# Moving some expert-weight loads from SyncE's DMA queue to ScalarE's in a two-layer hybrid backbone with a mixture of experts

## The chip, the cores and the metric

The kernel runs on one core of a Trainium2 chip. The metric is the device time of one execution, in microseconds (us). Five engines work side by side, each through its own list of instructions: TensorE (PE, matmuls), VectorE (DVE), ScalarE (ACT), GpSimd (POOL) and SyncE (SP, which here only issues DMA transfers). Semaphores order them against each other. DMA transfers are carried out by 16 DMA engines of the core; who issues a transfer decides through which queue it reaches them.

## The reference, cut to what matters

Two layers. Each is a token mixer (convolution, attention, RWKV-7 and retention heads, not touched here), then an expert-choice mixture of experts over 1024 latent tokens, and in the first layer over 256 context tokens as well. Everything is float32.

```python
def route_set(hs):
    aff = jax.nn.softmax((hs @ w_router + b_router).astype(jnp.float32), axis=-1)
    gate, idx = lax.top_k(aff.T, cap)              # 16 experts; cap = 128 latent tokens each
    xe = hs[idx]
    hid = jax.nn.silu(jnp.einsum('ecd,edf->ecf', xe, w_gate)) * jnp.einsum('ecd,edf->ecf', xe, w_up)
    ye = jnp.einsum('ecf,efd->ecd', hid, w_down) * gate[..., None].astype(hid.dtype)
    return jnp.zeros(hs.shape, ye.dtype).at[idx.reshape(-1)].add(ye.reshape(-1, hs.shape[-1]))
```

`w_gate`, `w_up` and `w_down` are 1024 x 1024 for each of 16 experts and each of two layers: 12 MB of weights for an expert, used once.

## The kernel before, in words

The work that the change touches is `stage_moe`, which runs once in each layer over the experts e = 0 to 15. An expert's three matrices are cut into quarters of 1 MB: g11, g12, g21, g22 of the gate matrix, u11 to u22 of the up matrix, d0 to d3 of the down matrix. All quarters pass through `g.moe_w`, a ring of 16 places in SBUF. `MOE_PARTS` lists them in the order of loading: for an expert g11, u11, g21, u21, g12, u12, g22, u22, and then d0 to d3 of the expert before. Part j goes to place j modulo 16, so it can be loaded only when part j - 16 has been used up. In steady state this gives, while expert e is computed: g12 and u12 of e+1 follow g11 and u11 of e; g22 and u22 of e+1 follow g21 and u21; d0 and d1 of e follow g12 and u12; d2 and d3 of e follow g22 and u22; and g11, u11, g21, u21 of e+2 follow d0 to d3 of e-1.

Gate and up projections are done with seven products of half-size blocks (Strassen-Winograd) in place of eight. TensorE runs them in the order P1, P2 | P6, P5, P7, P4, P3 (`first_products` and `other_products`, each product eight matmul pairs at L2915). The last reader of the quarters 11 is P5, of 12 is P7, of 21 is P4, of 22 is P3. Each product reads a gate and an up quarter at once, so both come free together. TensorE's list for expert e is: P6, four transposes, P5, four transposes of the next expert's tokens, P7, P4, P3, then P1 and P2 of expert e+1, then (first layer only) the context tokens' products of e+1, then eight transposes of the hidden rows of e (`hidden_turned`, L2958), then the down projection of e (L3014), which reads d0, d1, d2, d3 in this order.

ScalarE copies partial products and transposed tokens out of PSUM and applies SiLU (`gate`); VectorE forms the sums of weights and tokens that the products need (L3143, L3113), joins partial products (L3149) and multiplies gate and up (L3155). GpSimd gathers each expert's tokens and scatters its results with indirect DMAs.

Before the change every weight quarter is loaded by SyncE, in the order of `MOE_PARTS`, each behind a wait for its place:

```python
for j in range(RW, len(MOE_PARTS)):
    name, eo = MOE_PARTS[j - RW]
    if name[0] == "d":
        ...
    else:
        sp.wait_ge(*product_at(eo, {"11": P5, "12": P7, "21": P4, "22": P3}[name[1:]]))
    load_expert_part(sp, g, I, l, j)
```

The first 16 quarters of a layer are loaded by SyncE in `stage_topk`, ahead of this loop.

Of the kernel before, what the change touches and what calls it, by code (L numbers as in the profile page):

```python
# [86 lines left out]
def linker(eng, sig):  # L87

    def link(ins):
        ins.then_inc(*sig.up())  # L90
        eng.wait_ge(sig.sem, sig.made)
    return link
# [80 lines left out]
def row(v):  # L173

    return v.partition_broadcast(P)
# [2504 lines left out]
MOE_PARTS = [(name, e + d) for e in range(NE + 1) for name, d in MOE_ORDER if 0 <= e + d < NE]  # L2680
PART_AT = {part: j for j, part in enumerate(MOE_PARTS)}


def load_expert_part(sp, g, I, l, j):

    name, e = MOE_PARTS[j]
    half, c = divmod(int(name[1]), 2) if name[0] == "d" else (int(name[1]) - 1, int(name[2]) - 1)
    src = I[{"g": "w_gate", "u": "w_up", "d": "w_down"}[name[0]]][l, e].rearrange("(k p) f -> p k f", p=P)
    sp.dma_start(g.moe_w[:, j % MOE_RW], src[:, 4 * half:4 * half + 4, 512 * c:512 * c + 512]).then_inc(*g.sg(f"w_slot{j % MOE_RW}").up(16))  # L2689
# [75 lines left out]
def stage_moe(nc, g, I, l, need_ctx):  # L2765
# [4 lines left out]
    RW, w = MOE_RW, g.moe_w  # L2770
    A_, B_, C_, D_, CB, CD, YB = 0, 1, 2, 3, 4, 5, 6
    P1, P2, P6, P5, P7, P4, P3 = range(1, 8)
# [3 lines left out]
    with ExitStack() as cx:  # L2776
# [38 lines left out]
        def product_at(e, p):  # L2815

            return pm.at(7 * e + p)

        def joined_at(e, c):

            return cd.at(4 * e + c)
# [5 lines left out]
        def out_of(c):  # L2827

            return cb[:, {C11: 0, C12: 0, C21: 1, C22: 1}[c], {C11: 0, C21: 0, C12: 1, C22: 1}[c]]

        with nc.Block() as block:
            @block.sync
            def _(sp):
                sp.dma_start(rows[:], row(g.mod[l, 0, 5 * D:6 * D])).then_inc(*small.up(16))
                if need_ctx:
                    for q in range(4):
                        sp.dma_start(rowc[32 * q:32 * q + 32], g.mod[l, 1, 5 * D + 256 * q:5 * D + 256 * q + 256].partition_broadcast(32)) \
                            .then_inc(*small.up(16))
                for j in range(RW, len(MOE_PARTS)):
                    name, eo = MOE_PARTS[j - RW]  # L2840
                    if name[0] == "d":
                        if need_ctx:
                            sp.wait_ge(*dmc.at(eo + 1))
                        else:
                            sp.wait_ge(*dm.at(4 * eo + int(name[1]) + 1))
# [3 lines that stand above are left out]
# [182 lines left out]
            @block.scalar  # L3031
            def _(act):
                link = linker(act, achain)

                def x_copy(e, half):
                    act.wait_ge(*xtr.at(2 * e + half + 1))
                    nc.scalar.copy(xT[:, e % 2, 4 * half:4 * half + 4].rearrange("p k n -> p (k n)"), ps[:, C_]).then_inc(*xte.up())  # L3037

                def c_copy(e):
                    act.wait_ge(*xtrc.at(e + 1))  # L3040
                    nc.scalar.copy(xTc[:].rearrange("p k n -> p (k n)"), ps[:, CD, 256:256 + KT * CAPC]).then_inc(*xtec.up())

                def partial(e, p, i):
                    act.wait_ge(*product_at(e, p))
                    if p == P1 and e:
                        act.wait_ge(*joined_at(e - 1, C21))
                    if p == P6 and e:
                        act.wait_ge(*joined_at(e - 1, C12))
                    if p == P7:
                        act.wait_ge(*joined_at(e, C11))  # L3050
                    nc.scalar.copy(part[:, i], ps[:, A_]).then_inc(*tcd.up())  # L3051

                def gate(e, c):
                    act.wait_ge(*joined_at(e, c))
                    r, n = (0, 0) if c == C11 else (0, 1) if c == C12 else (1, 0) if c == C21 else (1, 1)
                    return nc.scalar.activation(hid[HF * r:HF * r + HF, 512 * n:512 * n + 512], out_of(c)[0:HF], ACT.Silu)

                def context_copy(e):
                    act.wait_ge(*cgu.at(e + 1))
                    nc.scalar.copy(gu[:], ps[:, CB]).then_inc(*cev.up())  # L3060

                def context_gate(e):
                    act.wait_ge(*ctr.at(e + 1))
                    if e:
                        act.wait_ge(*dmc.at(e))
                    nc.scalar.activation(hTc[:], ps[:, CB].rearrange("p (i q n) -> p i q n", i=4, q=4)[:, :, 0:2], ACT.Silu).then_inc(*cgs.up())

                x_copy(0, 0)
                x_copy(0, 1)
                if need_ctx:  # L3070
                    c_copy(0)
                partial(0, P1, 0)
                if need_ctx:
                    context_copy(0)
                    context_gate(0)
                for e in range(NE):
                    more = e + 1 < NE
                    partial(e, P6, 1)
                    if more:
                        x_copy(e + 1, 0)  # L3080
                        x_copy(e + 1, 1)
                        if need_ctx:
                            c_copy(e + 1)
                    partial(e, P7, 0)
                    gate(e, C11)
                    link(gate(e, C22))
                    link(gate(e, C21))
                    nc.scalar.copy(out_of(C21)[0:HF], out_of(C11)[HF:P]).then_inc(*hs.up())
                    gate(e, C12)
                    nc.scalar.copy(out_of(C22)[0:HF], out_of(C12)[HF:P]).then_inc(*hs.up())  # L3090
                    if more:
                        partial(e + 1, P1, 0)
                        if need_ctx:
                            context_copy(e + 1)
                    for half in range(2):
                        act.wait_ge(*htr.at(2 * e + half + 1))
                        nc.scalar.copy(hT2[:, 4 * half:4 * half + 4].rearrange("p k n -> p (k n)"), ps[:, C_ + half]).then_inc(*he.up())  # L3097
                    if more and need_ctx:
                        context_gate(e + 1)
# [226 lines left out]
```

## Time and profile before

| | |
|---|---|
| median of 3 runs | 4143.54 us (4136.83 to 4148.22) |
| the profiled execution's own time | 4128.93 us |
| its span | 4127.1 us |
| busy: PE, DVE, ACT, POOL | 3651.8, 2224.7, 1062.2, 491.2 us |
| experts' stage, first layer | about 1434 to 2228 us of the span |
| experts' stage, second layer | about 3489 to 4116 us of the span |
| weight quarters loaded in the two stages | 384 of 1 MB |

A row of the chain or of a timeline gives the start in us from the span's start, the length in us, and what ran; a bracket tells how long the engine had been idle before it and what ended that. "SPq" is SyncE issuing a DMA: its length is the time the issue took, not that of the transfer. The rows of a view of the DMA queues give how many packets each queue moved, their size, and the share that their time is of 16 engines' time; an issue's row ends with the us from issue to landing. Queue q1 holds what SyncE issues, q0 what GpSimd issues.

### The profile page before, as it was taken

What the parts mean: (1) busy time and instruction counts of PE and PEld (TensorE: products, weight loads), DVE (VectorE), ACT (ScalarE), POOL (GpSimd) and SP (SyncE); (2) the same over time, 40 slices, a digit from 0 to 9 for tenths busy, and PEclk for the clock granted to TensorE, in tenths of its full rate; (3) what the DMA queues carried; (4) which work ended last, traced back from release to release, by engine and by line L of the source; (5) the groups of instructions that cost most, each with busy time, mean ns of one, the idle gap of its engine ahead of it and who ended that gap; (6) DMA issues with size and microseconds to landing.
All of it is one profiled execution on the core that took longest, in us unless ns stands there. A gap on an engine that the chain in (4) does not pass through costs nothing. (4 is left out here: it accounts for less than half of the span.)

```text
span 4127.1 us, 65802 instructions
## 1 busy us (share of the span) xinstructions
PE 3651.8 (88%) x27258; PEld 2030.6 (49%) x27258; DVE 2224.7 (54%) x3676; ACT 1062.2 (26%) x2344; POOL 491.2 (12%) x675
## 2 busy tenths in 40 slices
PE   6899999677897699999997899998697875999998
PEld 4555575566733233333333655674486532333333
DVE  2454224687755644444443445334778757565654
ACT  3342010544311111111112443112534221212121
POOL 1100000221201011111111200000232110110100
PEclk8999999688998799999998899999698987999999
DMA  6300120200175677777774000121100326999996
GB/s 229 125 1 11 56 77 0 79 13 19 44 278 206 228 261 261 262 261 262 262 255 120 33 21 11 59 69 36 54 10 13 114 103 250 329 333 330 333 329 204
DMA packets 291447, 613.12 MB, mean 149 GB/s; under 512 B 37544, under 2 KB 45992, under 8 KB 284496
## 3 DMA queue, kind: packets, MB, share of 16 engines
q1 hardware_dynamic: 270608, 542.32, 36.9%
q0 software_dynamic: 20544, 66.60, 6.3%
q8 instruction: 219, 3.59, 0.4%
q14 instruction: 76, 0.62, 0.0%
HBM read 561.07 MB, written 47.79 MB: 148 GB/s over the span
## 5 line engine op out<-in xcount | busy, mean ns | idle before, releaser
L3014 PE MATMUL ps<-moe_w,e_hT 128*128 128x512 f32 x1024 | 451.1, 598 | 17.4 <-issue 9.2
L3143 DVE TENSOR_TENSOR moe_w<-moe_w 128x2048 f32<-128x2048 f32 x128 | 287.1, 2285 | 204.0 <-PE ps L2945 159.2
L2915 PE MATMUL ps<-moe_w,e_xs 128*64 128x512 f32 x1536 | 348.6, 596 | 0.8 <-DVE moe_w L3143 0.8
L2915 PE MATMUL ps<-moe_w,e_xT 128*64 128x512 f32 x1536 | 343.7, 597 | 0.7 <-DVE moe_w L3143 0.7
L3014 PEld LDWEIGHTS ps<-moe_w,e_hT 128*128 128x128 f32 x1024 | 192.9, 191 | 255.5 <-issue 252.7
L3149 DVE TENSOR_TENSOR e_cb<-e_part,ps 128x512 f32<-128x512 f32 x128 | 87.7, 685 | 335.2 <-ACT e_part L3051 249.3
L2915 PEld LDWEIGHTS ps<-moe_w,e_xT 128*64 128x64 f32 x1536 | 111.4, 138 | 221.3 <-issue 221.2
L2915 PEld LDWEIGHTS ps<-moe_w,e_xs 128*64 128x64 f32 x1536 | 105.4, 137 | 193.7 <-issue 192.3
L1207 PE MATMUL ps<-M 96*128 96x512 f32 (+1 forms) x400 | 182.6, 543 | 3.5 <-PEq L913 2.1
L3051 ACT COPY e_part<-ps 128x512 f32<-128x512 f32 x96 | 56.3, 586 | 479.8 <-PE ps L2915 471.5
L1097 PE MATMUL ps<-yT,hT 128*128 128x272 f32 (+1 forms) x608 | 146.6, 396 | 9.6 <-PEq L262 9.2
L659 ACT COPY yT<-ps 128x256 f32<-128x256 f32 (+1 forms) x90 | 42.5, 472 | 402.7 <-PE ps L571 402.7
L3143 DVE TENSOR_TENSOR moe_w<-e_t,moe_w 128x2048 f32<-128x2048 f32 x64 | 143.5, 2283 | 0.0
L1219 PEld LDWEIGHTS ps<-all_tabs,a_pr 128*128 128x128 f32 x656 | 74.7, 142 | 129.5 <-issue 88.2
L1097 PEld LDWEIGHTS ps<-yT,hT 128*128 128x128 f32 x608 | 114.7, 195 | 41.4 <-issue 20.0
L3143 DVE TENSOR_TENSOR e_t<-moe_w 128x2048 f32<-128x2048 f32 x60 | 134.5, 2283 | 0.0
L1219 PE MATMUL ps<-all_tabs,a_pr 128*128 128x128 f32 x656 | 111.9, 284 | 20.2 <-ACT a_pt L1268 13.8
L1268 DVE COPY a_pt<-ps 128x512 f32<-128x512 f32 (+1 forms) x104 | 61.1, 588 | 127.3 <-PE ps L1219 126.9
L2877 POOL DMA_INDIRECT x_rows<-e_ye,all_tok x16 | 52.6, 3290 | 641.1 <-DVE e_ye L3184 641.1
L1283 DVE TENSOR_REDUCE a_mx<-ps 128x1 f32<-128x1280 f32 (+1 forms) x72 | 98.4, 1367 | 52.2 <-PE ps L1207 52.2
L2877 POOL DMA_INDIRECT out_dram<-e_ye,all_tok x16 | 52.2, 3264 | 593.9 <-DVE e_ye L3184 593.9
L1310 ACT ACTIVATE a_pr<-ps,a_mx 128x1280 f32<-128x1280 f32 (+1 forms) x72 | 88.8, 1233 | 112.9 <-DVE a_mx L1284 112.9
(424 smaller groups left out, 7093.8 us busy)
## 6 DMA issues: line engine op xcount, KB each, us to landing
moe_w<-in_w_gate_dram SPq DMA_DIRECT2D x128, 1024.0 KB, 13.9
moe_w<-in_w_up_dram SPq DMA_DIRECT2D x128, 1024.0 KB, 14.1
moe_w<-in_w_down_dram SPq DMA_DIRECT2D x128, 1024.0 KB, 13.0
o_mod_w<-in_w_ada_dram SPq DMA_DIRECT2D x24, 1024.0 KB, 7.9
m_mod_w<-in_w_ada_dram SPq DMA_DIRECT2D x16, 1024.0 KB, 5.8
yT<-in_w_in_dram SPq DMA_DIRECT2D x6, 2048.0 KB, 7.9
r_z<-z_rows SPq DMA_DIRECT2D x20, 512.0 KB, 3.4
z_rows<-p_zo POOLq DMA_DIRECT2D x36, 256.0 KB, 2.3
```

The lines of the kernel that those rows point to most:

```text
L1097: ins = nc.tensor.matmul(ps[:, ZBANK[a], 0:hi - lo], hT[:, k, t * P:(t + 1) * P], w[:, k, lo:hi], start=(k == 0), stop=(k == KT - 1))
L1207: ins = nc.tensor.matmul(ps[:, SB[u % 2] + i, 0:w], QT[0:QK, h, t * P:(t + 1) * P], KTr[0:QK, h, n:n + w], start=True, stop=True)
L1219: ins = nc.tensor.transpose(ps[:, TB, k * P:(k + 1) * P], pr[:, u % NP, (k0 + k) * P:(k0 + k + 1) * P], g.ident)
L1268: copy(pt[:, k % 2, u % 2, k0:k0 + nk].rearrange("p k n -> p (k n)"), ps[:, TB, 0:nk * P]).then_inc(*done.up())
L1283: link(nc.vector.reduce_max(mx[:, s % 2, 0:1], src, AX_X))
L1310: nc.scalar.activation(pr[:, s % NP, 0:units[s][2] * P], src, ACT.Exp, bias=mx[:, s % 2, 1:2], scale=SCALE, accum_out=rs[:, s // 2 % 4, s ...
L2877: pool.indirect_dma_start(dst, bass.IndirectOffsetOnAxis(ap=g.tok[:, 0, e:e + 1], axis=0), ye[:], None, compute_op=ALU.add).then_inc(*sc.u ...
L2915: ins = nc.tensor.matmul(ps[HF * q:HF * q + HF, b, :], x[:, k], weights[q][:, k], start=(first and k == 0), stop=(k == 3), skip_group_chec ...
L3014: ins = nc.tensor.matmul(ps[:, YB + c, :], hT2[:, 4 * half + k], quarter(name, e)[:, k], start=(half == 0 and k == 0), stop=(half == 1 and ...
L3051: nc.scalar.copy(part[:, i], ps[:, A_]).then_inc(*tcd.up())
L3143: nc.vector.tensor_tensor(to, a, b, ALU.subtract).then_inc(*td.up())
L3149: nc.vector.tensor_tensor(out_of(c), part[:, 1 if c == C12 else 0], ps[:, b], ALU.subtract if c == C21 else ALU.add).then_inc(*cd.up())
```

## The change

SyncE's loop skips every part whose place was held by an up quarter. ScalarE issues those loads itself, at the point of its list where that quarter's last reader has run: `refill(e, "u11")` behind the copies of the next expert's transposed tokens, `refill(e, "u12")` behind the copy of P7, `refill(e, "u21")` behind the third SiLU, `refill(e, "u22")` behind the fourth. In steady state the loads moved are u12 and u22 of e+1 and d1 and d3 of e; d0, d2, all gate quarters and u11, u21 of e+2 stay with SyncE. These are 60 loads in each layer. No other work, buffer or size changes.

```diff
@@ SyncE's loop
                 for j in range(RW, len(MOE_PARTS)):
                     name, eo = MOE_PARTS[j - RW]
+                    if name[0] == "u":
+                        continue
                     if name[0] == "d":
@@ ScalarE's list
+                def refill(e, name):
+                    j = PART_AT[name, e] + RW
+                    if j < len(MOE_PARTS):
+                        act.wait_ge(*product_at(e, {"u11": P5, "u12": P7, "u21": P4, "u22": P3}[name]))
+                        load_expert_part(act, g, I, l, j)
+
@@
+                    refill(e, "u11")
                     partial(e, P7, 0)
+                    refill(e, "u12")
                     gate(e, C11)
                     link(gate(e, C22))
                     link(gate(e, C21))
+                    refill(e, "u21")
                     nc.scalar.copy(out_of(C21)[0:HF], out_of(C11)[HF:P]).then_inc(*hs.up())
                     gate(e, C12)
+                    refill(e, "u22")
                     nc.scalar.copy(out_of(C22)[0:HF], out_of(C12)[HF:P]).then_inc(*hs.up())
```

SyncE's list in the second layer, one expert in steady state, before. moe_w1 is the ring of quarters; signal29 counts the products of gate and up, signal11 those of the down projection. The loads are g12, u12, g22, u22, then d0 to d3, then g11, u11, g21, u21:

```order
L2689 DMA moe_w1<-in_w_gate_dram 128x4x512 [waits signal29]
L2689 DMA moe_w1<-in_w_up_dram 128x4x512 [waits signal29]
L2689 DMA moe_w1<-in_w_gate_dram 128x4x512 [waits signal29]
L2689 DMA moe_w1<-in_w_up_dram 128x4x512 [waits signal29]
L2689 DMA moe_w1<-in_w_down_dram 128x4x512 [waits signal29] x4
L2689 DMA moe_w1<-in_w_gate_dram 128x4x512 [waits signal11]
L2689 DMA moe_w1<-in_w_up_dram 128x4x512 [waits signal11]
L2689 DMA moe_w1<-in_w_gate_dram 128x4x512 [waits signal11]
L2689 DMA moe_w1<-in_w_up_dram 128x4x512 [waits signal11]
```

And now, the same expert: g12, g22, d0, d2, then g11, u11, g21, u21.

```order
L2689 DMA moe_w1<-in_w_gate_dram 128x4x512 [waits signal29] x2
L2689 DMA moe_w1<-in_w_down_dram 128x4x512 [waits signal29] x2
L2689 DMA moe_w1<-in_w_gate_dram 128x4x512 [waits signal11]
L2689 DMA moe_w1<-in_w_up_dram 128x4x512 [waits signal11]
L2689 DMA moe_w1<-in_w_gate_dram 128x4x512 [waits signal11]
L2689 DMA moe_w1<-in_w_up_dram 128x4x512 [waits signal11]
```

Behind g22 and ahead of d0 stood u22; it has left the list, as have u12, d1 and d3.

ScalarE's list in the second layer, one expert, now. e1_xT are the next expert's transposed tokens, e1_part partial products, e1_hid and e1_cb the hidden rows' halves; signal33 counts VectorE's joins:

```order
L3039 COPY e1_xT<-ps 128x512 [waits signal5] x2
L2689 DMA moe_w1<-in_w_up_dram 128x4x512 [waits signal29]
L3053 COPY e1_part<-ps 128x512 [waits signal33,signal29]
L2689 DMA moe_w1<-in_w_down_dram 128x4x512 [waits signal29]
L3058 ACTIVATE e1_hid<-e1_cb 64x512 [waits signal33] x2
L3058 ACTIVATE e1_hid<-e1_cb 64x512 [waits signal33,signal31]
L2689 DMA moe_w1<-in_w_up_dram 128x4x512 [waits signal29,signal31]
L3099 COPY e1_cb<-e1_cb 64x512
L3058 ACTIVATE e1_hid<-e1_cb 64x512 [waits signal33]
L2689 DMA moe_w1<-in_w_down_dram 128x4x512 [waits signal29]
L3102 COPY e1_cb<-e1_cb 64x512
```

The four DMA rows are new there (u12 of e+1, d1 of e, u22 of e+1, d3 of e); the other rows stood in the same order before, as L3037, L3051, L3056, L3088 and L3090.

## Rows read from the trace of the kernel before

**Rows 1.** The page: busy times and shares of the span.

```profile
PE 3651.8 (88%) x27258; PEld 2030.6 (49%) x27258; DVE 2224.7 (54%) x3676; ACT 1062.2 (26%) x2344; POOL 491.2 (12%) x675
```

**Rows 2.** Windows: experts' stages, second layer then first; clock, DMA share, GB/s last.

```profile
3488.70:4116.40 627.70, 617.45 (x2392) 235.54 (x2392) 365.46 (x281) 114.89 (x193) 67.42 (x28) 1.00 0.90 309
1434.30:2227.70 793.40, 786.71 (x4424) 307.14 (x4428) 376.38 (x311) 133.66 (x236) 99.39 (x56) 1.00 0.74 246
```

**Rows 3.** The chain in time: one of its steps through a d0, second layer.

```profile
3683.92 10.59 DMA moe_w<-in_w_down_dram
3694.64 13.97 PE ps L3014 x32
```

**Rows 4.** The down projection's line, second layer: idle time ahead of it.

```profile
  DMA moe_w<-in_w_down_dram: 4.3, 6
```

**Rows 5.** PE's timeline around P7, P4, P3 of one expert, second layer.

```profile
3675.83 3.65 PE L2915 MATMUL ps<-moe_w,e_xs 128*64 128x512 f32 x16
3679.31 3.60 PE L2915 MATMUL ps<-moe_w,e_xT 128*64 128x512 f32 x16
3682.74 3.60 PE L2915 MATMUL ps<-moe_w,e_xs 128*64 128x512 f32 x16
...
3693.15 1.09 PE L2958 MATMUL ps<-all_tabs,e_hid 128*128 128x128 f32 x8
```

**Rows 6.** SyncE's timeline, same expert: issues of weight loads.

```profile
3675.35 0.37 SPq L2689 DMA_DIRECT2D moe_w<-in_w_gate_dram  x1
...
3682.95 0.37 SPq L2689 DMA_DIRECT2D moe_w<-in_w_gate_dram  x1
...
3683.92 7.14 SPq L2689 DMA_DIRECT2D moe_w<-in_w_down_dram  x4
```

**Rows 7.** DMA issues, same expert: g12, u12, g22, d0, to landing.

```profile
moe_w<-in_w_gate_dram SPq DMA_DIRECT2D x1, 1024.0 KB, 8.3
moe_w<-in_w_up_dram SPq DMA_DIRECT2D x1, 1024.0 KB, 10.5
...
moe_w<-in_w_gate_dram SPq DMA_DIRECT2D x1, 1024.0 KB, 6.1
...
moe_w<-in_w_down_dram SPq DMA_DIRECT2D x1, 1024.0 KB, 10.6
```

**Rows 8.** ACT's and DVE's timelines, same expert.

```profile
3679.53 0.59 ACT L3051 COPY e_part<-ps 128x512 f32<-128x512 f32 x1 [3.01 <-PE ps L2915]
...
3683.74 0.63 ACT L3056 ACTIVATE e_hid<-e_cb 64x512 f32<-64x512 f32 x1 [2.18 <-DVE e_cb L3149]
...
3687.12 0.63 ACT L3056 ACTIVATE e_hid<-e_cb 64x512 f32<-64x512 f32 x1 [2.10 <-DVE e_cb L3149]
...
3688.41 0.69 DVE L3155 TENSOR_TENSOR e_hid<-e_hid,e_cb 128x512 f32<-128x512 f32 x1 [1.32 <-ACT e_cb L3090]
...
3697.67 4.48 DVE L3143 TENSOR_TENSOR e_t<-moe_w 128x2048 f32<-128x2048 f32 x2
```

**Rows 9.** The weight loads' line L2689, whole run.

```profile
L2689 SPq DMA_DIRECT2D moe_w<-in_w_up_dram x128: 495/1296/5985, 1328.9 to 4054.0; - x128
...
DMA to landing us min/median/max: 5.0/13.2/17.6
```

**Rows 10.** Two queues at once: queues in 1248:1251; landing times of L849 (POOL).

```profile
q1 hardware_dynamic: 102, 0.80, 65.4%
q0 software_dynamic: 101, 0.41, 33.5%
...
DMA to landing us min/median/max: 2.3/2.3/6.3
```

**Rows 11.** First layer: PE ahead of a down projection; d0's issue at 1469.46.

```profile
1487.07 13.97 PE L3014 MATMUL ps<-moe_w,e_hT 128*128 128x512 f32 x32 [0.28 <-issue]
...
moe_w<-in_w_down_dram SPq DMA_DIRECT2D x1, 1024.0 KB, 10.0
```

**Rows 12.** Window of TensorE's longest wait for d0: PE idle, clock, DMA.

```profile
3940.60:3942.30 1.70, 0.08 (x2) 0.06 (x1) 1.70 (x2) 0.72 (x2) 0.00 (x0) 1.00 1.05 386
```

## The prediction

> **What bounds the kernel now.** I read the page first: TensorE is busy for 88% of the span, no other engine for more than 54% [rows 1]. Then the windows of the two experts' stages, since the change touches nothing else. In the first layer's TensorE works 786.7 of 793.4 us and the DMA engines 74% of the time; in the second layer's it works 617.5 of 627.7 us and the DMA engines 90%, at 309 GB/s [rows 2]. Both are bound by TensorE, but in the second the transfers are close behind. The chain of waits says where they touch: in the second layer it leaves TensorE at one point only, through a down quarter, here from 3683.92 for 10.59 us and back into L3014 at 3694.64 [rows 3]. The down projection's line waited for w_down in six of its experts, 4.3 us together [rows 4]. So all that a better order of loads can give back there is about 4 us, 0.1% of the kernel, and the question is what the change does to d0, the first down quarter that TensorE asks for.
>
> One expert of the second layer, followed through PE's and SyncE's timelines. P5 ends at about 3675.3 and SyncE issues g12 at 3675.35. P7 runs from 3675.83 to 3679.4, P4 to 3682.9, P3 to 3686.3. SyncE gets to g22 when P4 is over, at 3682.95, and to d0 at 3683.92 [rows 5, 6]. The hidden rows' transposes start at 3693.15 and end at 3694.24, and the first matmul of L3014 could follow 0.3 us later [rows 5], a gap that the first layer shows with nothing to wait for, 0.28 us [rows 11]. So d0 is needed at 3694.5, which is 11.6 us after g22's issue. The landings: g12 at 3675.35 + 8.3 = 3683.7, u12 (issued some 0.4 us after g12) 10.5 later at 3686.3, g22 at 3689.1, d0 at 3694.5 [rows 6, 7]. With u22 between g22 and d0 the loads land 2.7 us apart: 1 MB each at 386 GB/s, which is what a window with the DMA engines full shows (share 1.05) [rows 12]. The shortest issue-to-landing time of a quarter is 5.0 us [rows 9], so 2.3 us pass around the 2.7 us of moving. In this expert the queue never ran dry between g12 and d0, and **d0 landed just when it was needed**. It is third in line behind g22 and u22; it has no slack. The 14 experts e = 1 to 14 of the second layer have the same order and the same distance of 11.6 us.
>
> **The change part by part.**
>
> *ScalarE's issues.* Sixty a layer. SyncE's issue of an up quarter takes 0.5 us at the least, 1.3 us in the median, 6.0 us at most, the long ones when its queue is full [rows 9]. ScalarE's queue holds at most two or three quarters at a time, so I take 0.5 us. What stands behind the issue of u22 is the copy L3088, and behind that of d3 the copy L3090, which VectorE's L3155 waits for. L3155 ended at 3689.1 and TensorE asked for its result at 3693.15 [rows 5, 8]: 4.0 us of cover in the second layer, and 7 us more in the first, where context products stand between. Four issues of 0.5 us cost nothing. If an issue blocked for 3 us it would still be covered; at 6 us it would cost 2 us an expert.
>
> *ScalarE's waits.* Each refill waits for a product that the instruction ahead of it has already waited for, directly or through a join, so nothing new is waited for. The u12 refill comes behind the copy of transposed tokens, one to two us later than SyncE issued it.
>
> *SyncE's list* loses u22 between g22 and d0. d0 is issued half a us sooner, which changes nothing while bytes are the limit.
>
> *The order of bytes* is what changes. d1 stood behind the wait for P4 and behind d0; now ScalarE issues it when P7 has been copied, 3679.53 + 0.59 = 3680.1 [rows 8]. Its data can flow from 3682.4, and it lies ahead of g22 and d0 in time. u22 goes from 3683.4 to the end of the third SiLU, 3683.74 + 0.63 = 3684.4, and d3 to 3687.12 + 0.63 = 3687.8 [rows 8]. So from 3685.2 (3682.95 + 2.3) on, SyncE's queue holds g22 and d0, 5.4 us of moving, and ScalarE's holds what is left of d1, then u22, then d3: never empty until d0 is in.
>
> What d0 gets of the DMA engines then decides. The trace has no two queues of 2 KB packets side by side, but it has SyncE's and GpSimd's. In 3 us where both had work the two moved 102 and 101 packets [rows 10]: **packet for packet, one for one**. Weight quarters have equal packets on both queues, so each gets half. Then d0 takes 2 x 5.4 = 10.8 us from 3685.2: it lands at 3696.0, or 13.1 us after g22's issue, against the 11.6 us at which it is needed. TensorE waits 1.5 us, 1.7 with the usual 0.15 us to start. That is the least by this rule. In the expert shown, g12 itself started late (it landed 8.3 us after issue, not 5.0), and sharing with u12 leaves about 0.55 us of it still to move at 3685.2, 1.1 us at half rate: 2.8 us of wait. Over the 14 experts I take 2.1 us, nearer to the low end since most start their g12 earlier. Sum: 14 x 2.1 = 29, less the 4.3 us waited now [rows 4], **+25 us**. d1 is by then there, and d2 and d3 are asked for 7 and 10.5 us after d0, when the queues have moved both.
>
> The Trainium skill ("DMA: Bandwidth & Descriptors", section "Queues, rings and completion order") says that each DMA engine goes round-robin between the queues it has work for, packet by packet; this trace agrees with its 102 to 101 packets. By that rule the sum is the one above.
>
> *VectorE's weight sums.* The t2 sums of e+1, which read g22 and u22, run from 3697.67 [rows 8]. At half rate g22 lands near 3691 to 3692 and u22 by 3697.5; the first of the two sums reads g22, the second, at 3699.9, u22. Covered.
>
> *First layer.* d0's issue at 1469.46 or just behind landed after 10.0 us, at about 1479.5, and TensorE began the down projection at 1487.07 [rows 11]: 7.5 us of slack, and DMA engines free a quarter of the time [rows 2]. A delay of 3 us is hidden. Zero.
>
> *The clock.* TensorE's longest wait for d0 now is 1.6 us, and the granted clock stayed at 1.00 (the 2.4 GHz level) in it [rows 12]; I put nothing for it.
>
> The profiled execution took 4128.9 us, 14.6 us (0.35%) under the median. Its sum is 4154 us; on the median, 4143.5 + 25 = 4168.5.
>
> **The rivals.**
>
> *A. Half shares, as above.* +18 to +35 us. Chance 0.53.
>
> *B. No slower: d0 does not suffer.* d0's queue now has one quarter ahead of it where there were two. If SyncE's queue is served first, or transfers are served in the order in which they were issued (d0 before u22), d0 lands at 3685.2 + 5.4 plus what is then left of u12 and d1, in this expert 1.1 + 2.7 us (u12 landed at 3686.3): 3694.4 at the latest, before 3694.5. All waits go, -4 us, which is within the noise. It decides as soon as ScalarE's queue gets less than a third of the engines while d0 moves. For it: GpSimd's stores of L849 land 2.3 us after issue alone but took up to 6.3 [rows 10] beside a load already under way, so a newcomer is not always served at once. Against it: the equal packets. 4139 to 4143 us, chance 0.26. The Trainium skill (same page, "Issuing engines are not separate DMA queues") says that issuing from several engines only saves the sequencer's time; taken alone, with transfers merely interleaved and no one's order mattering, it too would give no change. No run here shows two such queues yet.
>
> *C. Worse than half.* The same 6.3 against 2.3 us [rows 10] turned on d0: SyncE's queue is the newcomer at 3685.2, when d1 is under way. If g22 must wait until d1 is done, some 2 us in an expert whose g12 came in time, and only then gets half, the wait is 1.7 + 2 = 3.7 us: 14 x 3.7 - 4 = +48 us, 4191. Chance 0.12.
>
> *D. ScalarE blocks.* SyncE's issues last up to 6 us when its queue is full [rows 9]; were the unit behind both shared, d3's issue would hold L3090 and the hidden rows' transposes. 2 us for each of 14 experts, partly under d0's wait: +28 beyond A at most, 4180 to 4196. Chance 0.05.
>
> *E. Faster by over 0.3%* would need 12 us; the waits for loads hold 4. Chance 0.04, for what I don't see.
>
> **How the numbers follow.** I forecast A at its 2.1 us: 4168.5 us. The measurement tells about 0.3% (12 us) from no change. A, C and D are slower by more than that, save the low edge: 0.70. Same: B, 0.26. Faster: 0.04. The range takes in B's middle (4141) and C with some of its spread (4197); A alone is 4161 to 4179.
>
> **What would show it.** Right: in the second layer the line L3014 (with its new number) waits for w_down in 14 experts for 1.5 to 2.9 us each, some 30 us together; the stage grows from 628 to about 653 us and the first layer's stays at 793; d0's issue to landing rises from 10.6 to near 12.7 us while d1 lands before g22; and ScalarE's issues are 0.4 to 0.6 us long. B is right if d0 lands within 10 us and L3014 waits for nothing. D, if ScalarE's DMA rows are some us long and the transposes of the hidden rows wait for L3155. I would be wrong if the two queues don't share one for one, or if the loads move more per us from two queues than the 386 GB/s that one reached.

## The result and the profile after

The changed kernel takes 4207.98 us (median of 4 runs, 4200.94 to 4211.34) against 4140.18 us of the kernel before in the same runs: a ratio of 1.0174, with a 95% interval of 1.0152 to 1.0196. It is slower, as forecast, but by 68 us between the medians (72 by the ratio) where 25 were forecast, and it lies above the stated range. The profiled execution of the changed kernel took 4210.8 us, that of before 4128.9 us. Line numbers have moved: L3016 is the down projection (L3014 before), L2960 the hidden rows' transposes (L2958), L3099 and L3102 the copies (L3088, L3090).

The windows of the two experts' stages in the changed kernel, second layer first, which answer to [rows 2] (the last three columns are the granted clock, the DMA engines' share and GB/s), and three windows around one down projection of the second layer. A window's row gives its start and end, its length, then the busy time of PE, PEld (TensorE's weight loads), DVE, ACT and POOL, each with the number of instructions:

```profile
3494.30:4198.30 704.00, 646.62 (x2392) 246.35 (x2392) 365.63 (x282) 114.89 (x193) 67.43 (x28) 0.95 0.79 274
1430.10:2221.80 791.70, 785.02 (x4424) 306.50 (x4428) 376.43 (x311) 133.72 (x236) 99.42 (x56) 1.00 0.74 247
3766.70:3772.40 5.70, 2.28 (x14) 1.00 (x10) 4.40 (x2) 1.07 (x2) 0.00 (x0) 0.94 1.05 386
3772.40:3778.40 6.00, 5.92 (x7) 2.52 (x8) 6.00 (x4) 0.00 (x0) 0.00 (x0) 0.50 1.05 387
3778.40:3789.50 11.10, 11.10 (x28) 4.70 (x28) 2.93 (x3) 0.00 (x0) 0.00 (x0) 1.00 0.67 248
```

The first layer's stage is unchanged (793.4 before, 791.7 now). The second layer's went from 627.7 to 704.0 us, 76.3 of the 81.9 us between the two profiled executions; the other 5.6 us lie ahead of it, where the traces of the kernels below, the late d1 apart, differ by up to 10 us among themselves. The stage's loss has two parts, and the windows show both: the stage's idle time of TensorE went from 10.2 to 57.4 us, and its busy time, for the same 2392 matmuls, from 617.5 to 646.6 us. The idle time is one line's. The changed kernel's idle time ahead of L3016 in the second layer, against [rows 4]:

```profile
  DMA moe_w<-in_w_down_dram: 54.6, 14
```

Fourteen experts wait for d0 now, 3.9 us each on average (3.6 beyond the 0.3 us that always stand there [rows 11]), where six waited 4.3 us together. The busy time is the clock's. Read the three short windows above with TensorE's timeline of the same expert:

```profile
3757.49 3.60 PE L2917 MATMUL ps<-moe_w,e_xs 128*64 128x512 f32 x16
3760.92 7.04 PE L2917 MATMUL ps<-moe_w,e_xT 128*64 128x512 f32 x32
3767.89 1.09 PE L2960 MATMUL ps<-all_tabs,e_hid 128*128 128x128 f32 x8
3772.47 16.96 PE L3016 MATMUL ps<-moe_w,e_hT 128*128 128x512 f32 x32 [3.50 <-DMA moe_w<-in_w_down_dram]
```

TensorE was idle from 3768.97 to 3772.47. Then the granted clock is 0.50 (the 1.2 GHz level) for 6 us, in which 7 matmuls begin, and back at 1.00 (2.4 GHz) for the rest. The 32 matmuls take 16.96 us where they took 13.97 [rows 3]. So the stretch of 3.5 us is followed by 3.0 us more, lost at the lower clock.

What d0 waits for is read from the queues. SyncE's and ScalarE's issues for that expert (d0 and d2, then g11 of e+2; and u12, d1, u22, d3):

```profile
3758.11 3.39 SPq L2689 DMA_DIRECT2D moe_w<-in_w_down_dram  x2
3761.54 0.51 SPq L2689 DMA_DIRECT2D moe_w<-in_w_gate_dram  x1
```

```profile
3750.68 0.37 ACTq L2689 DMA_DIRECT2D moe_w<-in_w_up_dram  x1
...
3754.28 0.37 ACTq L2689 DMA_DIRECT2D moe_w<-in_w_down_dram  x1
...
3759.14 0.38 ACTq L2689 DMA_DIRECT2D moe_w<-in_w_up_dram  x1
...
3761.86 0.37 ACTq L2689 DMA_DIRECT2D moe_w<-in_w_down_dram  x1
```

ScalarE takes 0.37 us for each. u22 goes out when it was forecast, counted from the start of P7, and d1 and d3 some 0.6 us sooner: they are issued when the copy or SiLU ahead of them starts, not when it ends. The DMA issues of the same expert with their us to landing (d1, g22, d0), and then what each queue moved in three windows, 3759.5 to 3760.5, 3762 to 3762.5 and 3764 to 3768 (packets, MB, share of 16 engines' time; q1 is SyncE's, q10 ScalarE's):

```profile
moe_w<-in_w_down_dram ACTq DMA_DIRECT2D x1, 1024.0 KB, 8.7
...
moe_w<-in_w_gate_dram SPq DMA_DIRECT2D x1, 1024.0 KB, 9.2
...
moe_w<-in_w_down_dram SPq DMA_DIRECT2D x1, 1024.0 KB, 14.2
...
q10 hardware_dynamic: 191, 0.39, 104.9%
...
q1 hardware_dynamic: 92, 0.19, 102.0%
q10 hardware_dynamic: 4, 0.01, 3.3%
...
q10 hardware_dynamic: 384, 0.79, 53.3%
q1 hardware_dynamic: 383, 0.76, 51.5%
```

The last two rows are the mechanism that was forecast, as plainly as one could wish: 384 packets and 383. While both queues have work each gets half. d1 landed at 3763.0, g22 at 3766.9, d0 at 3772.3, 5.4 us after g22 and thus at exactly half of the rate of before, 2.7 us per MB. In all 14 experts d0 lands 5.3 to 5.4 us behind g22.

The rows above them show what was not in the sum. g22 was issued at 3757.7, but none of its packets moved up to 3760.5, 2.8 us later, while ScalarE's queue had all 16 engines (the first row). The forecast let g22 move from 2.3 us on, the time to report its end included. And the engines were not in step. A load has 16 marks of completion in the trace, one for each engine, and has landed when the last of them is through. d1's last packets were on one engine: three between 3762 and 3762.5, 0.17 us apart, where one engine moves six in that time (the fourth packet is another engine's mark that its part is done). That engine was thus shared one for one too, and SyncE's queue had the others. Read packet by packet, the first engine was through with its part of g22 at 3763.5 and the last at 3766.4. From 3760 to 3763 the two queues moved 357 and 225 packets, so g22 had more than its half in that time and still landed late, with the engine that was behind.

Part of this comes with GpSimd's queue (q0), which carries a gather of tokens for a later expert, issued 2.5 us before g12. What the queues moved from g12's issue to g22's, first in the expert above, then in the last of the 14, which has no such gather:

```profile
q1 hardware_dynamic: 520, 1.04, 39.6%
q0 software_dynamic: 212, 0.74, 35.2%
q10 hardware_dynamic: 350, 0.72, 25.0%
...
q1 hardware_dynamic: 528, 1.05, 43.4%
q10 hardware_dynamic: 587, 1.17, 40.1%
q0 software_dynamic: 60, 0.18, 12.3%
```

In that last expert g12 lands 5.4 us after its issue and g22 7.6, as half shares give it (7.7), and TensorE's idle stretch is 1.8 us. In the thirteen with the gather g12 takes 7.4 to 10.2 us, g22 8.5 to 11.2, and the stretches are 2.8 to 5.5 us. No run takes the gather away, so this is read from the trace and not tested.

### The profile page after: what moved, and what is told of

It is laid out like the page before. It is cut to its first block and busy times, and to the rows that moved or that the text cites. A ratio compares the mean times of both kernels' runs of the same rounds, so it can differ in the third digit from the quotient of the medians.

```text
span 4209.0 us, 65832 instructions
## 1 busy us (share of the span) xinstructions
PE 3683.3 (88%) x27258; PEld 2042.5 (49%) x27258; DVE 2226.7 (53%) x3676; ACT 1062.7 (25%) x2344; POOL 491.3 (12%) x675
## 5 line engine op out<-in xcount | busy, mean ns | idle before, releaser
L3016 PE MATMUL ps<-moe_w,e_hT 128*128 128x512 f32 x1024 | 478.5, 628 | 64.5 <-DMA moe_w<-in_w_down_dram 54.6
L3016 PEld LDWEIGHTS ps<-moe_w,e_hT 128*128 128x128 f32 x1024 | 203.2, 201 | 319.7 <-issue 317.0
L3196 DVE SCALAR_TENSOR_TENSOR e_ye<-ps,all_gate,e_rows 128x1024 f32<-128x1024 f32 x32 | 41.1, 1285 | 169.9 <-PE ps L3016 169.9
```

The lines of the kernel that those rows point to most:

```text
L3016: ins = nc.tensor.matmul(ps[:, YB + c, :], hT2[:, 4 * half + k], quarter(name, e)[:, k], start=(half == 0 and k == 0), stop=(half == 1 and ...
```

## The experiments

The theory after this reading, S: the loss is d0's lateness, made by the bytes that ScalarE's queue moves while d0 is due, and what TensorE's clock does after the wait. The rival, Q: two hardware queues cost by themselves, in proportion to what the second carries. Each kernel's ratio is to the kernel before on the same chip. The edits of the first three are to the changed kernel, and each gives one of ScalarE's loads back to SyncE, at its old place in the list.

**d1 back.**

```diff
-                    if name[0] == "u":
+                    if name in ("u11", "u21", "u22"):
...
-                    refill(e, "u12")
```

> The changed kernel, but d1 (the load behind u12) goes back to SyncE's list, behind d0; ScalarE keeps u12, u22 and d3. Theory S (half shares: d0 is late by the bytes that the other queue moves before it lands, d1 above all): with d1 gone from ahead of it, d0 has g22 and half of u22 and d3 in its way, as many bytes as in the kernel before, so the 3 to 5 us waits shrink to 0 to 2 us, the clock's drops with them, and the kernel takes 4140 to 4170 us. Rival Q (a second hardware queue costs by itself, whatever it carries): a quarter fewer loads there, a quarter of the loss back, 4190 us.

Measured: 4156.47 us, ratio 1.006 (1.0042 to 1.0078). TensorE's waits in the second layer (us in total, times, longest):

```profile
PE ps L3016 <- DMA moe_w<-in_w_down_dram: 24.4, 22, 2.0
```

One load moved back takes two thirds of the loss away. By TensorE's timeline only 5 of the 22 waits, 7.4 us, are for d0. The other 17.0 us are for d1 and, three times, d2, which now stand behind d0 in SyncE's queue.

**u22 back.**

```diff
-                    if name[0] == "u":
+                    if name in ("u11", "u12", "u22"):
...
-                    refill(e, "u21")
```

> The changed kernel, but u22 goes back to SyncE's list, between g22 and d0; ScalarE keeps u12, d1 and d3. Theory S: d0 now stands behind g22 and u22 in its own queue and still shares the engines with d1 and then d3, so more bytes than ever are moved before it: waits of 5 to 6 us against 3.8, the kernel slower than the changed one, 4220 to 4245 us. Rival Q: a quarter fewer loads on ScalarE's queue, 4190 us. The two differ in sign against the changed kernel.

Measured: 4217.33 us, ratio 1.0195 (1.0178 to 1.0212). The same view:

```profile
PE ps L3016 <- DMA moe_w<-in_w_down_dram: 73.6, 14, 6.4
```

ScalarE's queue carries a quarter less, and the 14 waits grow from 54.6 to 73.6 us, 5.3 each, as S says and Q cannot. In time the kernel is no faster than the changed one, and the two intervals overlap, so the sign rests on the waits; the time came out a little below the 4220 expected.

**d3 back.**

```diff
-                    if name[0] == "u":
+                    if name in ("u11", "u12", "u21"):
...
-                    refill(e, "u22")
```

> The changed kernel, but d3 goes back to SyncE's list, behind d2; ScalarE keeps u12, d1 and u22. Theory S: d3 is issued 4 us after d0 and lies behind u22 on ScalarE's queue, so it takes at most the last 1 to 2 us before d0 lands; without it d0 gets the full rate there: waits 0 to 1 us shorter, 4190 to 4208 us. Rival Q: 4190 us, as for any quarter of the loads.

Measured: 4168.58 us, ratio 1.0071 (1.0052 to 1.009).

```profile
PE ps L3016 <- DMA moe_w<-in_w_down_dram: 31.4, 14, 3.5
```

Both expectations missed; d3 costs more than either gave it, 1.7 us a wait. The reason lies in the landings: u22 lands some 3 us before d0 (3759.14 + 9.9 against 3772.3 in the expert above), so without d3 behind it d0 has the engines to itself for the last 3 us, which is worth half of that. I had given d3 only the last 1 to 2 us before d0 lands. This kernel also shows what waits of the forecast's size cost: 2.2 us each, and still TensorE's busy time in the stage was 633.8 us against 617.5 before, 16 us more at the lower clock:

```profile
3493.30:4161.20 667.90, 633.79 (x2392) 241.50 (x2392) 365.48 (x282) 114.85 (x193) 67.36 (x28) 0.97 0.83 288
```

**Only u12 moved** (the kernel before, with this one load on ScalarE's queue).

```diff
+                    if name == "u11":
+                        continue
...
+                    refill(e, "u11")
```

> The kernel before, with u12 of the next expert alone moved to ScalarE's queue. Theory S: g12 and u12 share the engines and are both in before g22 has started, so d0 lands when it did: within 0.3% of the kernel before, 4135 to 4150 us. Rival Q: a quarter of the loss, 4157 us.

Measured: 4140.52 us, ratio 0.9997 (0.9978 to 1.0016). TensorE's waits for down quarters in the second layer are 9.9 us in 6 times where 4.3 us stood before, which the time cannot tell. u12 lands 1.5 to 3.1 us after g22's issue in 13 of the 14 experts, about when g22's bytes begin to move, and costs next to nothing. After these four, Q has fallen: each is a quarter of the moved loads, and u12 alone costs nothing that the time shows, while taking back d1 gives two thirds of the loss, d3 more than half, and u22 nothing or less.

**One queue, d1 first.** Is it the queue, or only that d1 is moved ahead of g22?

```diff
-                for j in range(RW, len(MOE_PARTS)):
+                rank = ["g11", "u11", "u12", "g21", "g12", "u21", "g22", "u22", "d0", "d1", "d2", "d3"]
+                for j in sorted(range(RW, len(MOE_PARTS)), key=lambda j: (MOE_PARTS[j - RW][1] + (MOE_PARTS[j - RW][0][0] == "d"), rank.index(MOE_PARTS[j - RW][0]))):
```

> The kernel before, all loads on SyncE's queue, but in the order that the change gives to the bytes: g12, u12, then d1 as soon as P7 is over, then g22, d0, u22, d2, d3. Theory S (d0 is late because the second queue takes half the engines while d0 is due): on one queue d0 is still the third quarter counted from P4, d1 having taken u22's place, so it lands when it did and the time is that of the kernel before within 0.3%, 4125 to 4148 us. Rival O (moving d1 ahead of g22 is the harm, whatever the queue): waits of 2 us and more for d0, 4170 us or over.

Measured: 4130.9 us, ratio 0.9986 (0.997 to 1.0002). The order of issue that the change brought about does no harm on one queue: TensorE waits 2.7 us in all for down quarters. With two queues what stands behind d0 in time, u22's and d3's packets, is moved beside it.

**The filled wait.** The second part of the loss by itself: matmuls into the bank that the down projection overwrites, in TensorE's list just ahead of the wait for d0.

```diff
+                        if half == 0 and not need_ctx:
+                            for k in range(9):
+                                nc.tensor.matmul(ps[:, YB, :], g.ident, hid[:, 0:512], start=True, stop=True)
```

> The changed kernel, with nine matmuls of 128x512 into the bank that the down projection is about to overwrite, put in TensorE's list ahead of the wait for d0 in the second layer: about 4 us of work where TensorE stood idle for 3 to 5 us. The result is the same. Theory K (part of the loss is the clock, which falls to 1.2 GHz after these idle stretches and makes the 32 matmuls behind them take 15.7 to 17.0 us in place of 14.0, 31 us in all): the down projections return to 14.0 us, and the kernel takes some 20 to 30 us less than the changed one, 4178 to 4190 us, although TensorE does more. Rival: the slow matmuls are waits for d1 to d3 inside the group; then the filling changes nothing or adds to the time, 4208 us or more.

Measured: 4245.79 us, ratio 1.0259 (1.0225 to 1.0294). That lies in the rival's range, but the filling was twice as long as meant: TensorE's timeline shows 18 matmuls taking 7.96 us together in an expert. The down projections behind it took 13.9 us, as theory K has it; but in 8 us the later quarters come in too, so this run does not tell K from its rival.

**The filled wait, half as long** (`range(4)`).

> As the filled wait, but with four matmuls in place of nine: the nine took 7.9 us of TensorE an expert, twice what was meant, since each is carried out as two. Four take 3.5 us, about as long as the 3.6 us that TensorE stands idle for d0 in the changed kernel. The result is the same. Theory K (the clock, not more waits): the down projections return to 14.0 us (31 us in all gained over the changed kernel), the wait is filled and not lengthened, and the kernel takes 4175 to 4190 us. Rival: under 10 us gained, 4198 us or more.

Measured: 4186.53 us, ratio 1.0127 (1.0092 to 1.0163). TensorE's timeline of an expert, and the window of the stage:

```profile
3757.66 1.09 PE L2960 MATMUL ps<-all_tabs,e_hid 128*128 128x128 f32 x8
3759.08 3.67 PE L3014 MATMUL ps<-e_hid,all_tabs 128*128 128x512 f32 x8 [0.33 <-ACT e_hT L3112]
3762.59 13.90 PE L3019 MATMUL ps<-moe_w,e_hT 128*128 128x512 f32 x32
```

```profile
3496.10:4171.10 675.00, 667.61 (x2513) 257.23 (x2511) 361.94 (x279) 114.38 (x192) 67.38 (x28) 1.00 0.82 283
```

L3014 is the filling here and L3019 the down projection. TensorE does 3.5 us more in each expert, and the stage is 29 us shorter than the changed kernel's (675.0 against 704.0), with the clock at 1.00. d0 lands 0.5 to 3.9 us behind the hidden rows' transposes, 3.3 in the mean (1.7 to 5.4 and 3.8 in the changed kernel), and at most 0.1 us after the filling's end, so the wait is nearly as long as it was, only filled, and the later quarters have gained next to no time: the rival of K is out. The same 29 us are the growth of TensorE's busy time in the changed kernel (646.6 less 617.5). So 29 of the stage's 76 us were the clock's, and 47 the waits'. The time fell into the range that K gave; as ratios, 1.0127 against 1.0174, the two kernels' intervals overlap a little, and the traces carry the split.

**d1 late.** Half shares give waits of 2.1 us, and 3.6 to 3.9 were measured. Is the rest due to a load already under way when g22 comes?

```diff
-                    refill(e, "u12")
...
                     link(gate(e, C21))
+                    refill(e, "u12")
                     refill(e, "u21")
```

> The changed kernel, but ScalarE issues d1 4 us later, just ahead of u22: the same loads on the same queues, none of d1's bytes under way when SyncE's g22 comes. Theory N (what a half share did not explain, 2 us of 3.6, is that a queue that comes in while the other has a transfer under way is not served at once): waits for d0 of 0 to 1 us, 4135 to 4155 us. Rival H (half shares alone, and 2 us from some other cause that stays, such as one of the 16 engines lagging): taking d1's early bytes away is worth 1.5 us, so waits of about 2.1 us with the clock falling after most of them, 4170 to 4190 us.

Measured: 4245.32 us, ratio 1.0261 (1.0225 to 1.0296), outside both. The windows of the two stages, second layer first, and TensorE's longest wait in the first:

```profile
3592.60:4251.20 658.60, 626.02 (x2392) 236.12 (x2392) 365.40 (x281) 114.77 (x193) 67.36 (x28) 0.99 0.85 294
1430.00:2317.00 887.00, 818.91 (x4493) 313.43 (x4490) 379.77 (x318) 136.09 (x240) 99.34 (x56) 0.96 0.68 227
```

```profile
PE ps L2947 <- DMA moe_w<-in_w_up_dram: 61.8, 14, 5.3
```

They are two results. In the second layer the stage falls from 704.0 to 658.6 us, and the waits for d0 itself, counted from TensorE's timeline without the usual 0.3 us, to 4.9 us over the 14 experts, 0.35 each, where theory N had 0 to 1 and H 2.1. What is left there are twelve waits for d3, 20.8 us, now late in turn. g22 lands 5.9 us after its issue in the mean, where it took 9.6 in the changed kernel. But the 1.5 us that H gave to d1's bytes took ScalarE's load to start moving 2.3 us after its issue; its first packets came 3.8 us after. g22 then has the engines to itself for its whole 2.7 us, and half shares alone give it 2.7 us back. It gained 3.7 and d0 4.2, so 1.0 to 1.5 us of the gain are more than half shares explain, and N is borne out for that part only. In the first layer something new broke, which no one had in the expectation: u22, pushed behind d1 on ScalarE's queue, is late for the context products of the next expert (L2947), which read the raw quarters 22. These 61.8 us of waits and the lower clock behind them make the stage 95 us longer. Both theories took the first layer's slack, which I had read for d0, to hold for every load.

**The loads by time.** SyncE's list in the order in which the places come free (P5, P7, P4, P3), so that d0 goes out behind P7, once with all loads on one queue and once beside ScalarE's part as the change has it:

```diff
-                for j in range(RW, len(MOE_PARTS)):
+                rank = ["g11", "u11", "g12", "u12", "g21", "u21", "g22", "u22", "d0", "d1", "d2", "d3"]
+                for j in sorted(range(RW, len(MOE_PARTS)), key=lambda j: (MOE_PARTS[j - RW][1] + (MOE_PARTS[j - RW][0][0] == "d"), rank.index(MOE_PARTS[j - RW][0]))):
```

One queue:

> The kernel before, all on SyncE's queue, the loads issued in the order in which the places come free: behind P5 g12 and u12, behind P7 d0 and d1, behind P4 g22 and u22, behind P3 d2 and d3. d0 is then issued 3.5 us sooner and has nothing but d1 beside it. Theory S: all waits for d0 go; the second layer's experts take 623 to 625 us in place of 628 to 630 and the kernel gains 3 to 5 us, which 3 rounds can hardly tell: 4125 to 4145 us. Rival: the new order makes g22 and u22 late for VectorE's weight sums, or d2 late for TensorE: slower, 4150 us or more.

Measured: 4125.12 us, ratio 0.9979 (0.9955 to 1.0003); and again with more executions:

> The one-queue kernel by time once more, with five rounds, beside the kernel before: it waits for no load in the second layer, where the kernel before waits 3.5 to 4.3 us, so 0.1% is what the traces allow, 4125 to 4140 us; 0.3% and more, if the earlier ratio of 0.998 was no scatter.

Measured: 4126.21 us, ratio 0.9981 (0.9965 to 0.9997), barely clear of no change. In the first of the two TensorE waits for no load in the second layer, whose stage takes 624.1 us against 627.7; that accounts for 0.1% of the kernel:

```profile
3495.80:4119.90 624.10, 617.40 (x2392) 235.51 (x2392) 365.47 (x281) 114.77 (x193) 67.38 (x28) 1.00 0.89 308
```

Two queues:

> The changed kernel, ScalarE's part as it is, but SyncE's list in the order in which the places come free: g12, d0 (behind P7), g22, d2. d0 and d1 then go side by side. Theory S: two queues do no harm as long as d0 is issued early enough: d0 lands 2 to 3 us before it is needed, d2 shares with d3 and may be up to 1 us late: 4130 to 4155 us, against 4208 of the changed kernel. Rival Q (a second queue costs by itself): 4170 us or more.

Measured: 4128.16 us, ratio 0.9985 (0.9966 to 1.0003). With d0 issued 4 us earlier, the same traffic of ScalarE costs nothing; what TensorE still waits for is a later down quarter, 4.0 us in 7 waits.

**d0 in d1's place.** The sharpest form of the question: the changed kernel with two quarters' names exchanged, all else, bytes per queue and times of issue, the same.

```diff
-                    if name[0] == "u":
+                    if name in ("u11", "g12", "u21", "u22"):
...
-                        act.wait_ge(*product_at(e, {"u11": P5, "u12": P7, "u21": P4, "u22": P3}[name]))
+                        act.wait_ge(*product_at(e, {"u11": P5, "g12": P7, "u21": P4, "u22": P3}[name]))
...
-                    refill(e, "u12")
+                    refill(e, "g12")
```

> The changed kernel with two names exchanged: ScalarE loads d0 (into the place of g12) where it loaded d1, and SyncE loads d1 (into that of u12) where it loaded d0. Both queues carry the same number of bytes at the same times. Theory S (the loss is d0's lateness and what TensorE's clock does after it, nothing else): d0 lands when d1 did, 8 us before it is needed at the least 5, and d1 when d0 did, which is just about when TensorE asks for it, 3.5 us after d0: waits of 0 to 0.5 us for d1, 4130 to 4150 us. Rival Q (the traffic on two queues is the harm, whoever's bytes they are): the changed kernel's 4208 us, or over 4180.

Measured: 4135.69 us, ratio 0.9992 (0.9978 to 1.0007). TensorE's waits in the second layer:

```profile
PE ps L3016 <- DMA moe_w<-in_w_down_dram: 4.1, 9, 1.0
```

Nothing of the loss is left in the time. The transfers are as slow as they were: d1, now in d0's place, lands 2.5 to 4.9 us behind the transposes, 3.7 in the mean where d0 took 3.8. But TensorE asks for it one quarter, 3.5 us, later than for d0. Which quarter is behind the shared stretch is what counts.

## Why the prediction was wrong

**What bounds the kernel; d0 has no slack.** Right. The stage's loss is at L3016 of the second layer, in the 14 experts named.

**ScalarE's issues cost nothing.** Right: 0.37 us each, and L3102 ended at 3763.1, well ahead of the transposes at 3767.9. Rival D did not happen.

**The queues share packet for packet.** Right, 384 to 383. Rival B, that d0 would not suffer, fell with it. The Trainium skill ("DMA: Bandwidth & Descriptors", section "Issuing engines are not separate DMA queues") says that transfers issued by different engines interleave and that only issue time is saved. The trace agrees that they interleave. What the prediction had drawn from it, that nothing would change, failed: interleaving decides whose bytes are late, and here that cost 1.7%.

**2.1 us of wait an expert.** The first mis-sized term: 3.6 us beyond the usual gap were measured, near the 3.7 of rival C, though not by its way, that g22 moves nothing until d1 is done. The step that failed is "d0 takes 2 x 5.4 = 10.8 us from 3685.2", which has g22 in 7.7 us after its issue, and with it "nearer to the low end since most start their g12 earlier". d0's own 5.4 us at half rate were right in every expert. g22 landed 9.6 us after its issue in the mean. In the one expert without GpSimd's gather it was 7.6 us and the idle stretch 1.8 us, the least wait of the forecast; the other 13 have the gather beside g12, and there g22 landed 0.9 to 3.6 us later than in that one. That could be seen before: there too g12 takes 6.4 to 8.3 us in these 13 and 5.5 in the last. d1 under way adds to it, for with d1 late g22 landed 3.7 us sooner, 1.0 more than half shares give. How the excess divides between the gather and d1, and what delays a queue's first packets, stays open.

**The clock: nothing.** The second, and the step that was plainly wrong. I read from one wait of 1.6 us at a clock of 1.00 [rows 12] that waits of 2 us and more would leave the clock alone. One row of 1.6 us could not say that. In the changed kernel 13 of TensorE's 14 idle stretches ahead of L3016, those of 2.8 to 5.5 us, are followed by a down projection of 15.4 to 17.0 us, and the one of 1.8 us by one of 13.97. The filled wait measured it: 29 us. Waits of the size forecast would not have been free either: with d3 back they were 2.2 us each and cost 16 us of clock.

**The sum.** TensorE's idle time in the stage grew by 47 us, 14 x 3.6 less what was waited before within a us; with 29 us of clock it is 76, the stage's growth. Forecast were 25 and 0. That the time is slower was forecast for the right reason; the size missed by both terms.

**The first layer: zero.** Right for the change (791.7 us). The late d1 shows that u22 does not have the slack that was read for d0.

## What to carry to other kernels

When transfers already fill the DMA engines, a second queue gives no bandwidth; it takes half of the engines from whatever the first queue is moving. Before moving loads, find the one that lands just when it is needed and count everything that the other queue will have in flight until it lands; then issue that load first. And price a new wait of TensorE with what follows it: here 3.6 us of idling cost 2.2 us more in slow matmuls.

## What the runs showed of the hardware

The granted clock fell to its lower level after most of TensorE's idle stretches of 1.9 to 6.4 us: 0.94 in the window of the wait shown, 0.50 in the 6 us behind it, then 1.00. The length of the stretch alone does not decide it. In the kernel with d3 back, TensorE's timeline has

```profile
3580.48 15.67 PE L3016 MATMUL ps<-moe_w,e_hT 128*128 128x512 f32 x32 [1.89 <-DMA moe_w<-in_w_down_dram]
...
3800.73 13.97 PE L3016 MATMUL ps<-moe_w,e_hT 128*128 128x512 f32 x32 [2.58 <-DMA moe_w<-in_w_down_dram]
```

the slow one behind the shorter stretch; what else counts stays open. Two hardware queues of equal packets shared the engines 384 to 383, at the 386 GB/s that one queue reaches alone. Read packet by packet, SyncE's g12 moved its first packet 2.2 to 2.4 us after its issue, and ScalarE's u12, issued 0.6 us behind it, 3.3 to 3.7 us after its own. And a float32 matmul of 128x512 is carried out as two, 0.44 us each: the nine of the first filling show as 18 and took 7.96 us.
